# One indirect transfer per expert instead of one per pair of experts, with the 64 slots of an expert dealt in another order; and a wait of TensorE set behind a gate product

## The reference, cut to what matters

```python
def hierarchical_moe(xn, w_router_group, w_router_expert, w_expert_gate, w_expert_up, w_expert_down):
    t = xn.reshape(b * s, d)                       # 512 tokens of 1024 float32
    ...                                            # a group of 8 experts per token, the best 2 in it
    out = jnp.zeros_like(t)
    for e in range(N_EXPERTS):                     # 32
        hid = jax.nn.silu(t @ w_expert_gate[e]) * (t @ w_expert_up[e])
        out = out + combine[:, e:e + 1] * (hid @ w_expert_down[e])
```

## Time and profile before

| | us |
|---|---|
| median of 3 runs | 714.67 (713.92 to 717.95) |
| the profiled execution | 714.88 |
| its span, first to last instruction | 712.9 |
| mean granted clock of TensorE | 0.997 |

### The profile page before, as it was taken

How to read it: one execution, slowest core, us unless ns; L and a number is a source line. 1 busy time by engine, 2 the same in 40 slices (tenths; PEclk the granted TensorE clock), 3 DMA queues, 4 the chain that set the end, 5 groups by cost and what they waited for, 6 DMA issues and landing times.

```text
span 712.9 us, 10002 instructions
## 1 busy us (share of the span) xinstructions
PE 690.4 (97%) x3923; PEld 507.5 (71%) x3923; DVE 372.7 (52%) x725; ACT 254.7 (36%) x423; POOL 80.0 (11%) x116
## 2 busy tenths in 40 slices
PE   7999999999999999999999999999999999999794
PEld 6888988777777777788888888665555556555442
DVE  5378996667676868656446214852423221212227
ACT  7332134577676777544243211210111111111113
POOL 2000922000000101100003000011111112121000
PEclk9999999999999999999999999999999999999998
DMA  7523144322222111493406699699999999999983
GB/s 241 176 63 116 61 126 147 134 74 75 74 74 68 46 60 53 161 384 114 135 2 236 239 376 348 268 353 394 399 417 421 403 420 419 418 418 418 420 353 130
DMA packets 60360, 164.57 MB, mean 231 GB/s; under 512 B 7866, under 2 KB 39687, under 8 KB 47892
## 3 DMA queue, kind: packets, MB, share of 16 engines
q1 hardware_dynamic: 54820, 151.77, 56.1%
q0 software_dynamic: 5488, 12.11, 4.5%
HBM read 155.68 MB, written 16.00 MB: 241 GB/s over the span
## 4 chain that ended last, share of the span: by engine, by line
PE 90%; DMA 4%; DVE 4%; ACT 1%; issue 1%; SPq 0%; POOLq 0%; DVEq 0%; ACTq 0%
PE psum L1731 31%; PE psum L2155 15%; PE psum L1830 12%; PE psum L2181 8%; PE psum L2008 6%; PE psum L1842 3%; PE psum L2121 2%; DMA ring_e<-y_dram 2%; DVE ring_e L1093 2%; PE psum L1855 1%; PE psum L1884 1%; DMA y_dram<-ye,slots 1%; PE psum L2164 1%; PE psum L1967 1%; PE psum L1919 1%; PE psum L1907 1%
## 5 line engine op out<-in xcount | busy, mean ns | idle before, releaser
L1731 PE MATMUL psum<-xh,wh 128*128 128x512 f32 x256 | 99.9, 390 | 0.8 <-DVE xl L1093 0.8
L1731 PE MATMUL psum<-xl,wh 128*128 128x512 f32 x256 | 99.6, 389 | 0.0
L1731 PE MATMUL psum<-xh,wl 128*128 128x512 f32 x256 | 99.6, 389 | 0.0
L1096 DVE TENSOR_TENSOR wl<-raw,wh 128x1280 fp32r<-128x1280 f32 (+4 forms) x37 | 71.8, 1946 | 24.8 <-ACT wh L789 9.0
L1093 DVE SCALAR_TENSOR_TENSOR hid<-psum,rslot,act_g 128x256 f32<-128x256 f32 x17 | 8.2, 484 | 95.1 <-PE psum L2155 94.6
L1731 PEld LDWEIGHTS psum<-xh,wh 128*128 128x128 f32 x256 | 48.1, 188 | 11.1 <-DVE xl L1093 1.0
L1731 PEld LDWEIGHTS psum<-xh,wl 128*128 128x128 f32 x256 | 48.1, 188 | 9.9
L1731 PEld LDWEIGHTS psum<-xl,wh 128*128 128x128 f32 x256 | 48.1, 188 | 9.8
L1830 PE MATMUL psum<-xh,wh 128*128 128x512 f32 x128 | 51.3, 401 | 1.3 <-DVE k_fl L1093 1.3
L1830 PE MATMUL psum<-xh,wl 128*128 128x512 f32 x128 | 50.1, 391 | 0.0
L1830 PE MATMUL psum<-xl,wh 128*128 128x512 f32 x128 | 49.9, 390 | 0.0
(11 more groups left out here) (383 smaller groups left out, 1517.1 us busy)
## 6 DMA issues: line engine op xcount, KB each, us to landing
raw<-in_w_gate SPq DMA_DIRECT2D x16, 1024.0 KB, 6.4
raw<-in_w_in SPq DMA_DIRECT2D x9, 1024.0 KB, 5.5
ring_w<-in_w_expert_gate SPq DMA_DIRECT2D x8, 1024.0 KB, 20.4
ring_w<-in_w_expert_up SPq DMA_DIRECT2D x8, 1024.0 KB, 17.1
ring_h<-in_w_expert_down SPq DMA_DIRECT2D x8, 1024.0 KB
ring_h<-in_w_expert_gate SPq DMA_DIRECT2D x6, 1024.0 KB
ring_e<-in_w_expert_down SPq DMA_DIRECT2D x6, 1024.0 KB, 17.7
ring_e<-in_w_expert_gate SPq DMA_DIRECT2D x6, 1024.0 KB, 22.5
```

The lines of the kernel that those rows point to most:

```text
L1096: return dve.tensor_tensor(dst, src, hi.bitcast(F32), ALU.subtract)
L1731: last = nc.tensor.matmul(dst, a, b, start=start and n == 0, stop=stop and n == len(seq) - 1)
```

## The change

1. **Transfers.** `gather` and `scatter` issue two indirect transfers of 64 rows instead of one of 128. The first takes partitions 0 to 63, the second 64 to 127. The turn PART still has one. The second reads its indices from new tables `slots_b` and `toks_b`, which hold the second expert's indices on partitions 0 to 63. A turn's semaphore counts by 32 (HALVES), less 16 from PART on (`one_less`).
2. **Indices.** DVE makes the new tables: two more instructions in `slot_columns`, six in `exchange_columns`, two in `overflow_column`. POOL waits for both `idx_ready` counts before its first gather.
3. **Order of slots.** With a = 0 the ranks are dealt to d in the order 0, 2, 3, 1, with a = 1 in the order 2, 0, 1, 3, still back and forth over b.
4. **The wait.** The wait for "fk" moves from ahead of the first gate product to behind its 24 matmuls, ahead of the first branch product.

```diff
-                    for d in range(4):
-                        base, step = SLOT // 2 * a + 8 * d, 1
-                        if d % 2:
+                    for k, d in enumerate((2, 0, 1, 3) if a else (0, 2, 3, 1)):
+                        base, step = SLOT // 2 * a + 8 * k, 1
+                        if k % 2:
...
             def gather(c, i, s):
-                n, p = rows_of(c, i), column(c, i)
-                pool.indirect_dma_start(out=xg[n, s, :], out_offset=None, in_=x2_dram[:, :],
-                                        in_offset=bass.IndirectOffsetOnAxis(ap=toks[n, p], axis=0),
+                p = column(c, i)
+                pool.indirect_dma_start(out=xg[first, s, :], out_offset=None, in_=x2_dram[:, :],
+                                        in_offset=bass.IndirectOffsetOnAxis(ap=toks[first, p], axis=0),
                                         bounds_check=last_token, oob_is_err=False).then_inc(g_full[s], 16)
+                if whole(c, i):
+                    pool.indirect_dma_start(out=xg[second, s, :], out_offset=None, in_=x2_dram[:, :],
+                                            in_offset=bass.IndirectOffsetOnAxis(ap=toks_b[first, p], axis=0),
+                                            bounds_check=last_token, oob_is_err=False).then_inc(g_full[s], 16)
...
             def expert_pass(c):
-                pool.wait_ge(S["idx_ready"], c + 1)
+                pool.wait_ge(S["idx_ready"], c * 2 + 2)
...
+                dve.tensor_scalar(slots_b[0:SLOT, 0:NPAIR], table[0:SLOT, 1, :], float(UNUSED), None, ALU.add).then_inc(S["slots_in"], 1)
...
+                dve.tensor_scalar(toks_b[0:SLOT, 0:NPAIR], slots_b[0:SLOT, 0:NPAIR], 1, None, ALU.arith_shift_right).then_inc(S["idx_ready"], 1)
...
             def exchange_columns():
...
+                st.link(dve.tensor_copy(slot_f[first, :], slots_b[first, 0:NPAIR]))
+                exchanged(moved[first, :], slot_f[first, :], slot_f[first, OVER:OVER + 1], gap[first, :])
+                st.link(dve.tensor_copy(slots_b[first, FIXED:NPAIR], slot_f[first, FIXED:NPAIR]))
+                st.mark(dve.tensor_scalar(toks_b[first, FIXED:NPAIR], slots_b[first, FIXED:NPAIR], 1, None, ALU.arith_shift_right))
...
             def overflow_column():
...
+                st.link(dve.tensor_scalar(slots_b[first, NPAIR:NPAIR + 1], rs[first, 13, 0:1], float(UNUSED), None, ALU.add))
+                st.link(dve.tensor_scalar(toks_b[first, NPAIR:NPAIR + 1], slots_b[first, NPAIR:NPAIR + 1], 1, None, ALU.arith_shift_right))
...
-            for name in ("sq", "sk", "sv", "fq", "fk", "fv"):
+            for name in ("sq", "sk", "sv", "fq", "fv"):
                 evacuated(pe, name)
...
-            gates(PER_TILE)
+            gates(BEHIND_SCORES)
+            evacuated(pe, "fk")
+            gates(PER_TILE - BEHIND_SCORES)
```

More of the change, by code:

```diff
@@ L426, in halves, with one_less @@
             return row.rearrange("p (b n) -> p b n", b=2)
+        def one_less(s, i=PART):
+            return 16 if s == PART % 2 and i >= PART else 0
         def turn_no(c, i):
@@ L602, in _ @@
             for s in range(2):
-                sp_e.wait_ge(scattered[s], 16 * (NPAIR // 2 - s))
+                sp_e.wait_ge(scattered[s], HALVES * (NPAIR // 2 - s) - one_less(s))
             load_results(EARLY_ROWS)
@@ L630, in _ @@
                 for s in range(2):
-                    sp_e.wait_ge(scattered[s], 16 * (NPAIR // 2 * PASSES - s))
+                    sp_e.wait_ge(scattered[s], HALVES * (NPAIR // 2 * PASSES - s) - one_less(s))
                 load_results(range(NT))
@@ L717, in turn, with whole @@
                 pool.sem_inc(S["turns"], 1)
-            def rows_of(c, i):
-                return slice(0, SLOT if isinstance(c, int) and i == PART else P)
+            first, second = slice(0, SLOT), slice(SLOT, P)
+            def whole(c, i):
+                return not (isinstance(c, int) and i == PART)
             def gather(c, i, s):
-                n, p = rows_of(c, i), column(c, i)
-                pool.indirect_dma_start(out=xg[n, s, :], out_offset=None, in_=x2_dram[:, :],
-                                        in_offset=bass.IndirectOffsetOnAxis(ap=toks[n, p], axis=0),
+                p = column(c, i)
+                pool.indirect_dma_start(out=xg[first, s, :], out_offset=None, in_=x2_dram[:, :],
+                                        in_offset=bass.IndirectOffsetOnAxis(ap=toks[first, p], axis=0),
                                         bounds_check=last_token, oob_is_err=False).then_inc(g_full[s], 16)
+                if whole(c, i):
+                    pool.indirect_dma_start(out=xg[second, s, :], out_offset=None, in_=x2_dram[:, :],
+                                            in_offset=bass.IndirectOffsetOnAxis(ap=toks_b[first, p], axis=0),
+                                            bounds_check=last_token, oob_is_err=False).then_inc(g_full[s], 16)
             def scatter(c, i, s):
-                n, p = rows_of(c, i), column(c, i)
-                pool.indirect_dma_start(out=y_dram[:, :], out_offset=bass.IndirectOffsetOnAxis(ap=slots[n, p], axis=0),
-                                        in_=ye[n, :], in_offset=None, bounds_check=last_row,
+                p = column(c, i)
+                pool.indirect_dma_start(out=y_dram[:, :], out_offset=bass.IndirectOffsetOnAxis(ap=slots[first, p], axis=0),
+                                        in_=ye[first, :], in_offset=None, bounds_check=last_row,
                                         oob_is_err=False).then_inc(scattered[s], 16)
+                if whole(c, i):
+                    pool.indirect_dma_start(out=y_dram[:, :], out_offset=bass.IndirectOffsetOnAxis(ap=slots_b[first, p], axis=0),
+                                            in_=ye[second, :], in_offset=None, bounds_check=last_row,
+                                            oob_is_err=False).then_inc(scattered[s], 16)
             def expert_pass(c):
@@ L1535, in overflow_column @@
             def overflow_column():
-                second = slice(SLOT, P)
+                first, second = slice(0, SLOT), slice(SLOT, P)
                 dve.wait_ge(S["slot_ps"], 3)
@@ L1602, in expert_pass @@
                     dve.wait_ge(S["slot_ps"], 1)
-                    slot_columns(2, bank[3])
+                    slot_columns(3, bank[3])
                     st.link(dve.tensor_copy(rc[:, 0, :], bank[3][:, 320:320 + NE]))
@@ L1706, in _ @@
                     for s in range(2):
-                        dve.wait_ge(scattered[s], c * (NPAIR // 2 * 16) - s * 16)
+                        dve.wait_ge(scattered[s], c * (NPAIR // 2 * HALVES) - s * HALVES - one_less(s))
                     all_slot_hits()
@@ L1710, in _ @@
                     dve.wait_ge(S["rs_ps"], c + 2)
-                    slot_columns(c * 2 + 2, bank[7])
+                    slot_columns(c * 3 + 3, bank[7])
                     slot_norms(c + 2)
@@ L2118, in x_transposes @@
                 elif b == 0:
[L2119 removed]
+                    pe.wait_ge(g_full[s], (i + 1) // 2 * HALVES - one_less(s, i) if isinstance(c, int) else c * (NPAIR // 2 * HALVES) + (i // 2 + 1) * HALVES - one_less(s))
                 for k in range(4 * b, 4 * b + 4):
```

13 lines of the change are left out of this document (8 added, 5 removed).

## The result

The changed kernel takes 723.16 us (median of 4 runs, 723.03 to 723.54); the kernel before takes 715.28 beside it. The ratio is 1.0106, with a 95% interval of 1.0076 to 1.0137: slower by 1.1%, where I had forecast 710.4 us and a range that ended at 714.4. The profiled execution took 723.54 us, its span is 721.8 (before: 712.9).

What follows compares the result with a forecast made beforehand. PE was taken to bound the kernel until turn 14 of the experts, DMA traffic the last 45 us. Span 712.9 - 3.0 - 1.3 = 708.6 us, 710.6 with 1.98 around it, less 0.2: 710.4; range 709.0 to 714.4.

Steps and rivals of the forecast that it cites:

- Two transfers of 64 rows, new order of slots: gain 3.0 us: Experts' gathers and scatters: rows spread evenly over 16 DMA engines, so the tail's last loads land 3.0 us earlier.
- The fade of the DMA share: End of the weights' traffic: last load 5.3 us behind the mean engine, 3.0 of it from uneven rows, to be removed.
- A: Rival, chance 0.23: splitting transfers brings no balance, only the wait's 1.3 us remains, 713.4 us.
- B: Rival, chance 0.05: four consecutive partitions share an engine, so the busy engines end 7.6 us later, 721.0 us.
- The mapping of the engines: Indirect transfers: 128 partitions give each half eight engines (1117 and 812 rows); 64-row transfers use all 16, two partitions each.
- Latency of a scatter: Experts' turns: the split scatter lands after 8.9 us instead of 7.9, hidden within the 10.7 us a turn leaves.
- DVE's index steps: Turn 2 of the experts: added index instructions delay `hid` and cost PE about 0.65 us, hidden by later slack.
- The moved wait: First gate product: PE no longer idles for `k_fl`, gain 1.3 us, bounds 0.7 and 1.5.
- What is late next: Tail, turn 15: last up product ends at 683.2, DVE's additions at 684.2, so its row load is late by 1.0 us.

## Why the prediction was wrong

**The failed step** is "Two transfers of 64 rows, new order of slots: gain 3.0 us". The fade of the DMA share is shorter by 2.8 us, as forecast, but no run shows that as time: with both directions balanced and no loss on the weights the kernel takes 713.04 us (`hid` comes later there too), with the moved wait alone 712.57. What is missing is a cost in the same step, which I had put at nothing without a reason: I priced a gathered row at 0.156 us on its engine wherever it lands, and took the weights' 421 GB/s as given. A gather wholly in one half takes a quarter to two fifths of the rate away while its rows land. That is 13.4 us over the experts' turns, and it turned -4.3 into +8.9 in the span. Between the two kernels that differ by the gathers' partitions and the deal, it is 725.34 - 711.14 = 14.2 us. The trace of before had the price: turn 8's gather costs 0.66 us; 30 more of them would be 20 us, 21 us if it goes by rows (958 more, 0.66 us for 30). Against the 13.4 measured, that is too much, but it gives the sign. I used turn 8's scatter to learn how 64 rows spread over the engines and never looked at what its gather did to its neighbours.

**The rivals.** A (the split buys nothing) I had weighed low, since the rule behind it speaks of full transfers. It also missed the sign. B's 721.0 us lies near the 723.16 measured by luck: it wanted a longer fade, and the fade got shorter. None of my rivals had a transfer slow down others. The Trainium skill has a rule that fits a part of what the runs show (SBUF — State Buffer, Door 1: The DMA port swizzle): a transfer's partitions reach the memory's 16 DMA ports by bits of their number, and 64 partitions from 0 or from 64 reach only half of them. The trace agrees in the drop (254 to 315 GB/s beside 0 to 63, 426 and 430 beside 32 to 95). By the ports alone, though, turn 13's rows, all in the lower half, would crowd as well, and they don't. One reading would be that only a transfer wholly in one half is dealt to all 16 engines, so that engines write into the ports of others. The profile names no engines and no ports, and no run tests it: it is a guess, and why such a gather slows the rest stays open.

**The mapping of the engines.** That a contiguous 64-row transfer goes over all 16 agrees with the tail of the changed kernel (2.5 us instead of 5.3). The router's counts give 1119 and 810 rows for the two halves, not 1117 and 812, which changes no term by more than 0.1 us. And the DMA engines were full from slice 27 on, not 26.

**Latency of a scatter.** Right: the second half of turn 14's, issued 1.23 us after the first, landed 7.44 us later, 8.7 us in all; forecast 8.9. The copies into `ye` wait for it a little (ACT 9.9 us in 4 turns), PE doesn't.

**DVE's index steps.** Forecast 0.65 us in turn 2. `hid` starts at 503.05 there, 0.8 us earlier than in the earlier trace rows, with a head start of 1.45: 0.65 us lost, right.

**The moved wait.** Right: 1.45 us at the start of the experts' part where 1.3 were forecast, and measured alone -0.3%.

**What is late next.** Here a second step failed, hidden behind the first. I let PE's turns shrink to "the steps between" and took the end of the last up product as 683.2. Without the loss (gathers into every second partition, both split) the last weights came when forecast, but about half of the turns grew by 0.5 us, and the time was 713.04 instead of 710.4. The changed kernel has these waits too (`hid` 5.7 us in 9 waits, 2.0 in 2 before). So even with the first cost taken away the forecast would have been 2.6 us too good.

## What to carry to other kernels

Before splitting a transfer, ask what the pieces do to the traffic beside them, and look for one such piece in the trace already: turn 8's single gather and the GB/s beside it would have given the sign here. A DMA share of 1.0 says that the engines are busy; only the rate says what they move. If a gather must be split, let each part span both halves of the partitions, by columns or by every second one; of the kernels measured here that compute the trunk's result the moved wait, with or without split scatters, is the best, 0.3 to 0.5% ahead of the kernel before. It isn't told apart from the gathers split by columns (0.9973).

## What the runs showed of the hardware

- Beside a gather into partitions 0 to 63 the DMA rate fell from some 418 to between 238 and 332 GB/s, at a full share, and beside one into 64 to 127 to 270 to 291; beside gathers into 32 to 95 and into every second partition it stayed at 410 to 430.
- Scatters, which read from 64 neighbouring partitions, cost the weights nothing (415.4 GB/s with all of them split).
- A second gather that moves no row is free for the others (415.1 GB/s). Twice as many gathers with row packets of half the size are nearly so (414.4).
- With four indirect transfers a turn instead of three, the next step behind PE's product came 0.5 us later in about half of the turns. The cause is open.
